# Two decays placed ahead of a weight rounding on ScalarE, and the second head sum of each pair placed behind the chunk's low products on TensorE

## Chip, cores, metric

One core of a Trainium2 chip runs the whole program. The metric is the device time of one execution in microseconds. TensorE (PE) does the matrix products, VectorE (DVE), ScalarE (ACT) and GpSimd (POOL) the rest, SyncE (SP) starts most transfers. Each engine takes its instructions strictly in the order in which the program gives them to it; between engines only semaphores order the work.

## What is computed

Two blocks, one after the other, on 1024 tokens of width 1024. The change touches only the first block, which has two layers:

```python
def hybrid_layer(x, ...):
    h = rms_norm(x, pre_gain) * (1.0 + scale) + shift
    proj = h @ w_in                     # 24 chunks of 128 columns, and a gate of rank 16
    (aq, ak, av, ag, rq, rk, rv, rg, gq, gk, gv, gg, ga) = jnp.split(proj, IN_SPLITS, axis=-1)
    a_out = sliding_window_attention(aq, ak, av, sinks) * jax.nn.silu(ag)
    r = retention(rq, rk, rv)
    r_out = rms_norm(r) * jax.nn.silu(rg)
    log_a = jax.nn.log_sigmoid(ga @ gla_gate_w + gla_gate_b) / 16
    g = gated_linear_attention(gq, gk, gv, log_a)
    g_out = rms_norm(g, gla_norm_gain) * jax.nn.silu(gg)
    y = jnp.concatenate([a_out, r_out, g_out], axis=-1) @ w_out
    return x + gate * rms_norm(y, post_gain)
```

The second block (attention over a window and a context, a gating unit, a Fourier mix and a wide feed-forward part) is not touched.

## The kernel before

**Units and chunks.** The first block runs as four units (`it` 0 to 3: two layers by two halves of 512 tokens). A unit goes through 32 weight chunks of 128 output columns: chunks 0 to 23 are the input projection, 24 to 31 the output projection. The products are made in a split float32 form: the raw chunk (`wraw`) is rounded on ScalarE to `whi` (`split_high`, line 620), GpSimd makes the rest `wlo` (`split_low`, line 523), and the PE makes three passes: `whi` with `h_hi` and with `h_lo` (`high_products`, line 1160, 16 matmuls of 512 columns), then `wlo` with `h_hi` (`low_products`, line 1168, 8 matmuls). "The third pass" of the change is `low_products`. `wraw`, `whi`, `wlo` and the result banks `lin0`, `lin1` have two places each, so a chunk's rounding waits until the PE has made the high products of the chunk two before (`hi_used`). Chunks 2 and 3, and 6 and 7, are made in pairs by `token_half` (line 1183): the first half in step 2, the second, with the release of both chunks, in step 3.

**The mixers.** Between the passes stand small steps of attention, retention and gated linear attention (GLA), placed by hand through a number `at`: position `2*s` stands ahead of chunk `s`, position `2*s+1` in its middle, between its high and its low products on the PE. On ScalarE the order of one step `s` is: `mixers(2s)`, `refill(s)` (the rounding of chunk `s+2`; at `s` = 3 of chunks 4 and 5, at `s` = 2 nothing), `mixers(2s+1)`, `evacuate(s)` (the result bank to SBUF, which frees it). Each engine has its own `mixers` function with the same numbers.

**Around the first part of the change (step 3 of a unit).** `log_decay` on ScalarE (position 4) and `log_sums` on VectorE (position 5) give `bsum`, the running sum of the gate's logarithms. GpSimd's `distance(0)` and `distance(1)` (position 6, line 538) write differences of it to `zed`. ScalarE's `decay(lv)` (lines 671 and 672) takes absolute value and exponential of `zed`; GpSimd's `keys(lv)` (line 549) and VectorE's `queries(lv)` (line 920) multiply with it, and the PE's `level(lv)` (line 1241) multiplies keys with queries. `level(0)` stands at position 8, between the modulation products of step 4 (`mod_products`, line 187) and the high products of chunk 4. Those wait also for ScalarE's evacuation of the bank of step 3 (line 768).

**Around the second part (steps 15, 16 and 19, 20).** The four 128-wide parts of the retention and GLA outputs are normalized over each head. `head_squares` makes squares. On the PE `head_sum(n)` (line 1335, one float32 matmul of 512 columns, recorded as two) sums them over a head into the single bank `bankM`. ScalarE's `head_root(n)` reads it with a logarithm (line 643); for odd `n` two exponentials follow (line 648), which need another activation table. VectorE's `head_scale` (line 967) multiplies, for both parts of a pair, at the odd position. `HEAD_SUM_AT = [30, 31, 38, 39]`: the first of a pair ahead of chunk 15 (19), the second in its middle. `head_sum(1)` may write `bankM` only when ScalarE has read the first sum (`head_log`). `mod_step` at the head of step 16 (20) writes `bankM` too, and waits for the logarithm of the second sum:

```python
if n in (0, 2):
    pe.wait_ge(*mod_out.after(it * mod_groups + HEAD_SUM_AT[n] // 8, 1))
else:
    pe.wait_ge(*head_log.after(it, n))
```

On VectorE `denominator` (line 992), which GpSimd's `normalized` (line 565) and then the PE's `turn_probs` in the middle of the next chunk (line 1364) wait for, stands behind the `head_scale` steps. ScalarE's `exponentials` (attention, position 30 and 38) stand ahead of `head_root`.

Of the kernel before, what the change touches and what calls it, by code (L numbers as in the profile page):

```python
# [38 lines left out]
LOGIT_AT, DIAG_AT = 4, 6  # L39
# [8 lines left out]
HEAD_SUM_AT = [30, 31, 38, 39]  # L48
# [317 lines left out]
def first_block(nc, t, a, sem):  # L366

    with ExitStack() as ctx:
# [99 lines left out]
        def group_of(it, s):  # L468

            return it * mod_groups + s // 4  # L470
# [140 lines left out]
        def _(act):  # L611
# [46 lines left out]
            def log_decay(it):  # L658

                l = it // NB  # L660
                act.wait_ge(*logit_done.after(it, 1))
                act.wait_ge(*h_ready.after(it, KB))
                link(nc.scalar.activation(zed[:, 0, :], four[0], ACT.Identity, bias=cols1[:, l, C_GB:C_GB + 1]))
                link(nc.scalar.activation(zed[:, 1, :], zed[:, 0, :], ACT.Abs))
                link(nc.scalar.activation(zed[:, 1, :], zed[:, 1, :], ACT.Exp, scale=-1.0))
                nc.scalar.activation(zed[:, 1, :], zed[:, 1, :], ACT.Ln, bias=1.0).then_inc(*sig_ready.one)
# [47 lines left out]
            def mixers(it, at):  # L714

                if at == LOGIT_AT - 1:
                    act.wait_ge(*ga_done.after(it, 1))
                    nc.scalar.activation(ga[:], bankE[0:2 * GATE_RANK, :], ACT.Copy).then_inc(*ga_ready.one)
                if at == LOGIT_AT:
                    log_decay(it)  # L720
                if at == DIAG_AT + 1:
                    decay(it, 0)
                    decay(it, 1)
                if at in LEVEL_AT:
                    lv = LEVEL_AT.index(at)
                    if lv + 2 <= LEVELS:
                        decay(it, lv + 2)
                    if lv == 2:
                        nc.scalar.activation(eb, bsum[:], ACT.Exp).then_inc(*eb_ready.one)
                        nc.scalar.activation(elast[:], bsum[:, P - 1::P], ACT.Exp).then_inc(*eb_ready.one)  # L730
                if at in FINAL_AT:
                    gla_final(it, FINAL_AT.index(at))
                if at == FINAL_AT[-1] + 2:
                    act.wait_ge(*g_evac.after(it, NT))
                    head_squares(it, 0)
                if at in RET_AT[1:]:
                    m = RET_AT.index(at) - 1
                    act.wait_ge(*r_out.after(it, m + 1))
                    nc.scalar.activation(rq[:, :, m * P:(m + 1) * P], bankE[:, 0:256].rearrange("p (c n) -> p c n", n=P),
                                         ACT.Copy).then_inc(*r_evac.one)  # L740
                if at == RET_AT[-1] + 2:
                    act.wait_ge(*r_evac.after(it, NT))
                    act.wait_ge(*kh_done.after(it, NT))
                    head_squares(it, 2)
                if at in SCORE_AT:
                    exponentials(it, SCORE_AT.index(at))
                if at in HEAD_SUM_AT:
                    head_root(it, HEAD_SUM_AT.index(at))
                if at == V_AT:
                    act.wait_ge(*v_turned.after(it, 1))  # L750
                    act.wait_ge(*carried.after(it, 1))
                    nc.scalar.activation(av[:, 1:, :].rearrange("p t n -> p (t n)"), bankE[:], ACT.Copy).then_inc(*v_ready.one)
                if at in TURN_AT:
                    transposed(it, TURN_AT.index(at))
# [52 lines left out]
            for it in range(UNITS):  # L807
# [19 lines left out]
                for k in range(KB):  # L827
                    s = OUT1 + k
# [321 lines left out]
        def _(pe):  # L1150
# [13 lines left out]
            def low_products(it, c):  # L1164

                pe.wait_ge(*w_split.after(it, c + 1))
                for k in range(KB):
                    last = nc.tensor.matmul(bank[c % 2], wlo[:, c % 2, k * P:(k + 1) * P], h_hi[:, k, :],  # L1168
                                            start=False, stop=(k == KB - 1))
                last.then_inc(*lin_done.one)  # L1170
# [157 lines left out]
            def head_sum(it, n):  # L1328

                pe.wait_ge(*head_sq_ready.after(it, n + 1))  # L1330
# [4 lines that stand above are left out]
                nc.tensor.matmul(bankM[:], ones64[:], head_sq[HEAD_ORDER[n]], start=True, stop=True).then_inc(*head_summed.one)  # L1335
# [56 lines left out]
            def mod_step(it, s):  # L1392

                g = group_of(it, s)
                if s % 4 < 2:
                    if s % 4 == 0 and g:
                        pe.wait_ge(*mod_out.after(g - 1, 1))
                        for n in (1, 3):
                            if s == HEAD_SUM_AT[n] // 2 + 1:
                                pe.wait_ge(*head_log.after(it, n + 1))  # L1400
                    for c in (2 * (s % 4), 2 * (s % 4) + 1):
                        pe.wait_ge(mod_in[c], 16 * (g + 1))
                        mod_products(nc, bankM, c * P, cact, mod_ring, c).then_inc(*mod_summed.one)
                elif s in FOLD_AT:
                    pe.wait_ge(*mod_row_ready.after(g, 1))
                    fold_products(nc, bankM[:, 0:4 * VEC * MOD_GROUP], t["fold"][:], mod_row[:]).then_inc(*mod_turned.one)

            def mixers(it, at):

                if at == 2:  # L1410
                    gate_rank(it)
                if at == LOGIT_AT:
                    pe.wait_ge(*ga_ready.after(it, 1))
                    nc.tensor.matmul(four[0], t["gate_w"][:, it // NB, :], ga[:], start=True, stop=True).then_inc(*logit_done.one)
                if at == DIAG_AT:
                    diagonal(it)
                if at in LEVEL_AT:
                    level(it, LEVEL_AT.index(at))
                if at in FINAL_AT:
                    gla_final(it, FINAL_AT.index(at))  # L1420
                if at in RET_AT:
                    retention(it, RET_AT.index(at))
                if at in HEAD_SUM_AT:
                    head_sum(it, HEAD_SUM_AT.index(at))
                if at == V_AT:
                    turn_values(it)
                if at in SCORE_AT:
                    score(it, SCORE_AT.index(at))
                if at in TURN_AT:
                    turn_probs(it, TURN_AT.index(at))  # L1430
                if at in VALUE_AT:
                    values(it, VALUE_AT.index(at))

            x_summed(0)
            for it in range(UNITS):
                for s in range(OUT1):
                    mod_step(it, s)
                    mixers(it, 2 * s)
                    if s in (GV, RV):
                        token_half(it, s, 0)  # L1440
                    elif s in (GV + 1, RV + 1):
                        token_half(it, s - 1, 1)
                    else:
                        high_products(it, s, when=(lambda k: h_ready.after(it, k + 1)) if s == 0 else None)
                        if it and s == 0:
                            y_summed(it - 1)
                        mixers(it, 2 * s + 1)
                        low_products(it, s)
                mod_step(it, OUT1)
                mixers(it, 2 * OUT1)  # L1450
                for c in range(2):
                    pe.wait_ge(*lin_free.after(it, OUT1 + c + 1))
                    pe.wait_ge(*w_split.after(it, OUT1 + c + 1))
                    out_products(it, c, MIX_ORDER[:4])
                mod_step(it, OUT1 + 1)
                for c in range(2):
                    out_products(it, c, MIX_ORDER[4:])
                for k in range(2, KB):
                    mod_step(it, OUT1 + k)
                    if k == 5:  # L1460
                        x_summed(it + 1)
                    if k < KB - 1:
                        high_products(it, OUT1 + k)
                        low_products(it, OUT1 + k)
                    else:
                        last_products(it, OUT1 + k)
# [1730 lines left out]
```

## Time and profile before

| | before |
|---|---|
| median of 3 runs | 4014.93 us |
| lowest and highest | 4013.55, 4018.3 us |
| the profiled execution, whole time | 4015.34 us |
| its span, first to last instruction | 4013.6 us |
| PE busy | 93% of the span |
| mean granted clock of the PE | 0.97 |
| first block, four units | about 76 to 1243 us of the span |

All times below are microseconds from the start of the span. An engine's idle time stands in a row in brackets, with the engine and line that ended it. PEclk is the PE's granted clock: 1.00 is 2.4 GHz, and where it falls it falls to 1.2 GHz for a stretch.

### The profile page before, as it was taken

To read this page: it belongs to the slowest core of one execution; us is meant where nothing else is said; L and a number is where in the kernel's file an instruction comes from. 1 tells how busy PE (TensorE), PEld (TensorE's weight loads), DVE (VectorE), ACT (ScalarE), POOL (GpSimd) and SP (SyncE) were. 2 spreads that over 40 slices of the span, in tenths; PEclk is the share of its full clock that TensorE was granted. 3 is DMA by queue.
4 is the path that set the end of the run, shared out by engine and by line. 5 is a ranking of instruction groups with operands and counts; after the bars stand their busy time and mean duration, and the time that the engine had idled before them with its cause. 6 is when DMAs were issued, how large, how long until landed. Compare 5 with 4: busy or idle time off the path is not lost.

```text
span 4013.6 us, 61376 instructions
## 1 busy us (share of the span) xinstructions
PE 3716.5 (93%) x22388; PEld 2993.7 (75%) x22388; DVE 2118.4 (53%) x3355; ACT 1726.9 (43%) x2899; POOL 1779.6 (44%) x1288
## 2 busy tenths in 40 slices
PE   4999999999998899888999999999899899999997
PEld 3767767767766677657888898887777778887886
DVE  5546546546546567667324655236667574235234
ACT  2355355355355544555223454235444553233223
POOL 1543544434443522325455885454322355455444
PEclk7999999999999899998999999999999999999999
DMA  6333433433333321212232453322221223232323
GB/s 252 122 124 125 138 118 126 146 111 134 127 122 109 103 82 48 64 53 87 91 98 92 145 173 110 94 94 79 85 84 53 63 79 94 89 96 96 94 92 103
DMA packets 127222, 421.32 MB, mean 105 GB/s; under 512 B 17281, under 2 KB 19105, under 8 KB 126369
## 3 DMA queue, kind: packets, MB, share of 16 engines
q1 hardware_dynamic: 121488, 410.09, 31.1%
q10 hardware_dynamic: 5520, 8.34, 0.6%
q8 instruction: 140, 2.29, 0.2%
q14 instruction: 74, 0.60, 0.0%
HBM read 397.40 MB, written 6.29 MB: 101 GB/s over the span
## 4 chain that ended last, share of the span: by engine, by line
PE 54%; DVE 7%; ACT 3%; issue 2%; POOL 0%; DMA 0%; SPq 0%; ACTq 0%; DVEq 0%; POOLq 0%
PE lin L2672 30%; PE lin L2681 15%; PE bankO L2797 2%; PE lin L2930 2%; PE bankT L2739 2%; DVE x L2317 1%; DVE tmp L2283 1%; DVE y L2316 1%; PE scores L2772 1%; DVE h_lo L2306 1%; DVE staged L2295 1%; PE lin L2814 1%; ACT whi L1902 0%; PE lin L2702 0%; PE scores L2773 0%
## 5 line engine op out<-in xcount | busy, mean ns | idle before, releaser
L1883 POOL TENSOR_TENSOR wlo<-late_raw,whi 128x512 fp32r<-128x512 f32 x456 | 641.2, 1429 | 764.4 <-PE lin L2681 497.6
L1883 POOL TENSOR_TENSOR wlo<-wraw,whi 128x512 fp32r<-128x512 f32 x452 | 635.9, 1431 | 716.8 <-PE lin L2681 497.5
L2672 PE MATMUL lin<-h_hi,whi 128*128 128x512 f32 (+1 forms) x1896 | 715.2, 384 | 47.4 <-ACT f L2196 12.4
L2672 PE MATMUL lin<-h_lo,whi 128*128 128x512 f32 (+1 forms) x1896 | 701.1, 377 | 0.0
L523 POOL TENSOR_TENSOR wlo<-wraw,whi 128x512 fp32r<-128x512 f32 x260 | 359.5, 1404 | 464.6 <-PE lin L1168 290.2
L2672 PE MATMUL lin<-a_hi,whi 128*128 128x512 f32 (+1 forms) x1280 | 471.9, 376 | 12.0 <-ACT tmp L2205 7.8
L2672 PE MATMUL lin<-a_lo,whi 128*128 128x512 f32 (+1 forms) x1280 | 468.7, 374 | 0.0
L2672 PEld LDWEIGHTS lin<-h_hi,whi 128*128 128x128 f32 x1896 | 368.2, 194 | 133.5 <-issue 24.9
L1902 ACT ACTIVATE whi<-late_raw 128x1024 fp32r<-128x1024 f32 x228 | 239.2, 1057 | 517.2 <-PE lin L2672 414.9
L1902 ACT ACTIVATE whi<-wraw 128x1024 fp32r<-128x1024 f32 x226 | 237.3, 1057 | 497.0 <-PE lin L2672 413.3
L2681 PE MATMUL lin<-h_hi,wlo 128*128 128x512 f32 (+1 forms) x1896 | 439.8, 375 | 1.2 <-POOL wlo L1883 0.8
L2672 PEld LDWEIGHTS lin<-h_lo,whi 128*128 128x128 f32 x1896 | 368.7, 194 | 61.1 <-issue 1.2
L2681 PEld LDWEIGHTS lin<-h_hi,wlo 128*128 128x128 f32 x1896 | 334.0, 190 | 66.6 <-issue 6.2
L2550 DVE TENSOR_TENSOR tmp<-tmp 128x512 f32<-128x512 f32 (+1 forms) x160 | 185.3, 1158 | 335.3 <-ACT tmp L2205 330.2
L1160 PE MATMUL lin<-h_hi,whi 128*128 128x512 f32 x800 | 334.9, 419 | 10.5 <-DVE h_lo L869 10.5
L1160 PE MATMUL lin<-h_lo,whi 128*128 128x512 f32 x800 | 323.4, 404 | 0.0
L2681 PE MATMUL lin<-a_hi,wlo 128*128 128x512 f32 (+1 forms) x1280 | 296.9, 376 | 2.1 <-POOL wlo L1883 2.1
L2672 PEld LDWEIGHTS lin<-a_hi,whi 128*128 128x128 f32 x1280 | 241.9, 189 | 67.2 <-ACT tmp L2205 15.7
L2672 PEld LDWEIGHTS lin<-a_lo,whi 128*128 128x128 f32 x1280 | 242.0, 189 | 46.2 <-issue 0.2
L620 ACT ACTIVATE whi<-wraw 128x1024 fp32r<-128x1024 f32 x130 | 136.7, 1057 | 302.6 <-PE lin L1160 206.6
L2576 DVE TENSOR_TENSOR y<-lin,y 128x512 f32 (+1 forms) x96 | 66.4, 692 | 378.4 <-PE lin L2681 378.2
L2681 PEld LDWEIGHTS lin<-a_hi,wlo 128*128 128x128 f32 x1280 | 226.7, 190 | 51.3 <-POOL wlo L1883 3.4
(381 smaller groups left out, 6435.4 us busy)
## 6 DMA issues: line engine op xcount, KB each, us to landing
wraw<-in_w SPq DMA_DIRECT2D x332, 512.0 KB, 3.5
late_raw<-in_w SPq DMA_DIRECT2D x212, 512.0 KB, 3.5
mod_ring<-in_w_ada SPq DMA_DIRECT2D x96, 512.0 KB, 4.6
mod_ring<-in_w_mod SPq DMA_DIRECT2D x32, 512.0 KB, 4.6
tmp<-tmp SPq DMA_DIRECT2D x224, 64.0 KB, 2.0
first_ring<-in_w_mod SPq DMA_DIRECT2D x16, 512.0 KB, 16.6
wraw<-in_dft_tokens SPq DMA_DIRECT2D x16, 512.0 KB, 3.5
late_raw<-in_dft_tokens SPq DMA_DIRECT2D x16, 512.0 KB, 3.5
```

The source lines that it names most:

```text
L523: last = nc.gpsimd.tensor_tensor(wlo[:, s, half], wraw[:, s, half], whi[:, s, half].bitcast(F32), ALU.subtract)
L620: nc.scalar.activation(whi[:, s, :], wraw[:, s, :], ACT.Copy).then_inc(*w_hi.one)
L1160: last = nc.tensor.matmul(bank[c % 2], whi[:, c % 2, k * P:(k + 1) * P], h[:, k, :], start=(k == 0 and h is h_hi), stop=False)
L1883: last = nc.gpsimd.tensor_tensor(wlo[:, s, half], raw_chunk[r][:, half], whi[:, s, half].bitcast(F32), ALU.subtract)
L1902: nc.scalar.activation(whi[:, s, 0:D], raw_chunk[r], ACT.Copy).then_inc(*w_hi.one)
L2550: nc.vector.tensor_tensor(tmp[:, 2 + s, 0:w], tmp[:, 4 + s, 0:w], tmp[:, 4 + s, 0:w], ALU.mult).then_inc(*a_sq.one)
L2576: nc.vector.tensor_tensor(part, bank[s][:, 0:p.w], part, ALU.add).then_inc(*lin_free.one)
L2672: last = nc.tensor.matmul(bank[s][:, 0:p.w], whi[:, s, k * P:(k + 1) * P], h[:, k, 0:p.w], start=(k == 0 and h is parts[0]), stop=False)
L2681: last = nc.tensor.matmul(bank[s][:, 0:p.w], wlo[:, s, k * P:(k + 1) * P], parts[0][:, k, 0:p.w], start=False, stop=(k == KB - 1))
L2739: last = nc.tensor.transpose(out, probs[i % 2][:, kv, k * P:(k + 1) * P], ident[:])
L2797: last = nc.tensor.matmul(bankO[half, g * P:(g + 1) * P], v, probsT[:, kv, at:at + P], start=(k == 0), stop=(k == n - 1))
L2930: return nc.tensor.matmul(bank[c][:, 0:2 * P].rearrange("p (t n) -> p t n", t=2), x_part[:, k, cols], w[:, 0:2, k * P:(k + 1) * P], start= ...
```

## The change

Three lines of order are changed, nothing of what is computed. On ScalarE `decay(it, 0)` and `decay(it, 1)` move from position 7 to position 6 of a unit, that is from behind the rounding of chunks 4 and 5 to ahead of it. On the PE the second `head_sum` of each pair moves from the middle of chunk 15 (19) to behind that chunk's low products. At position 39 `turn_probs` and `values` of attention stand in the middle of the chunk as before.

```diff
@@ ScalarE, mixers
-                if at == DIAG_AT + 1:
+                if at == DIAG_AT:
                     decay(it, 0)
                     decay(it, 1)
@@ TensorE, mixers
-                if at in HEAD_SUM_AT:
+                if at in HEAD_SUM_AT[::2]:
                     head_sum(it, HEAD_SUM_AT.index(at))
@@ TensorE, the loop over the chunks
                         mixers(it, 2 * s + 1)
                         low_products(it, s)
+                        if 2 * s + 1 in HEAD_SUM_AT:
+                            head_sum(it, HEAD_SUM_AT.index(2 * s + 1))
```

## Rows read from the trace of the kernel before

**Rows 1.** The page's first part: busy time, share, instructions of each engine.

```profile
PE 3716.5 (93%) x22388; PEld 2993.7 (75%) x22388; DVE 2118.4 (53%) x3355; ACT 1726.9 (43%) x2899; POOL 1779.6 (44%) x1288
```

**Rows 2.** Waits of the PE in 80 to 1240: total us, times, longest.

```profile
PE bankM L1335 <- ACT tmp L643: 19.7, 8, 2.5
PE bankM L195 <- DVE mod_row L1050: 14.9, 8, 2.9
PE quad L1241 <- POOL big L549: 11.1, 4, 2.8
```

**Rows 3.** Timeline of ScalarE, unit 1, step 3: start us, us, line, operation.

```profile
395.94 2.00 ACT L620 ACTIVATE whi<-wraw 128x1024 fp32r<-128x1024 f32 x2 [7.27 <-PE lin L1183]
397.86 0.62 ACT L671 ACTIVATE big<-big 128x512 f32<-128x512 f32 x1
398.49 1.28 ACT L672 ACT_TABLE_LOAD   x1
...
400.96 0.63 ACT L672 ACTIVATE big<-big 128x512 f32<-128x512 f32 x1
401.50 1.07 ACT L768 ACTIVATE gv<-lin 128x512 f32<-128x512 f32 x2
```

**Rows 4.** Timeline of GpSimd and VectorE in the same stretch.

```profile
392.32 2.07 POOL L538 TENSOR_TENSOR big<-bsum 128x512 f32<-128x512 f32 x2 [5.21 <-DVE bsum L900]
...
400.49 0.73 POOL L549 TENSOR_TENSOR big<-gk,big 128x256 f32<-128x256 f32 x1 [6.09 <-ACT big L672]
400.52 2.39 DVE L920 TENSOR_TENSOR tmp<-gq,big 128x256 f32<-128x256 f32 x2 [4.74 <-ACT big L672]
```

**Rows 5.** Timeline of the PE: unit 1's modulation products, unit 0's first product of chunk 4.

```profile
397.75 1.08 PE L187 MATMUL bankM<-mod_ring,cact 128*32 128x128 f32 x32
...
113.03 0.50 PE L1160 MATMUL lin<-h_hi,whi 128*128 128x512 f32 x1
```

**Rows 6.** Busy times by stretch (stretch, length, engines, PEclk, DMA share, GB/s), level(0) to level(1); last row level(2) to level(3).

```profile
111.98:118.50 6.52, 6.52 (x49) 5.06 (x49) 3.59 (x3) 2.23 (x4) 6.52 (x6) 0.74 0.24 83
401.60:409.28 7.68, 7.68 (x48) 6.10 (x49) 4.02 (x3) 2.23 (x4) 7.68 (x8) 0.61 0.22 73
...
983.19:989.66 6.47, 6.47 (x48) 5.04 (x48) 3.54 (x3) 2.23 (x4) 6.47 (x6) 0.74 0.22 81
122.61:127.52 4.91, 4.91 (x52) 3.90 (x48) 2.77 (x2) 1.88 (x4) 4.91 (x6) 1.00 0.45 114
```

**Rows 7.** Timeline of all engines around unit 0's first pair of head sums.

```profile
220.94 0.60 ACT L643 ACTIVATE tmp<-bankM 128x512 f32<-128x512 f32 x1
221.44 1.05 ACT L620 ACTIVATE whi<-wraw 128x1024 fp32r<-128x1024 f32 x1
...
221.68 1.10 PE L1335 MATMUL bankM<-tmp,ones 128*128 128x512 f32 x2 [2.47 <-ACT tmp L643]
...
222.22 2.42 PE L1168 MATMUL lin<-h_hi,wlo 128*128 128x512 f32 x8
...
222.82 0.60 ACT L643 ACTIVATE tmp<-bankM 128x512 f32<-128x512 f32 x1 [0.33 <-PE bankM L1335]
...
224.57 1.08 PE L187 MATMUL bankM<-mod_ring,cact 128*32 128x128 f32 x32
...
227.37 1.89 POOL L565 TENSOR_TENSOR big<-big,rden 128x1024 f32<-128x1024 f32 x1 [11.27 <-DVE rden L995]
...
230.43 1.04 PE L1364 MATMUL quad<-ident,big 128*128 128x128 f32 x8
```

**Rows 8.** Busy by stretch: second pairs, the same without head sum, unit 0's first pair.

```profile
258.66:267.60 8.94, 6.48 (x27) 4.07 (x27) 1.73 (x5) 6.74 (x11) 0.00 (x0) 0.81 0.24 99
...
1131.43:1140.48 9.05, 6.59 (x28) 4.14 (x27) 2.31 (x5) 6.75 (x11) 0.75 (x1) 0.81 0.00 0
273.44:277.46 4.02, 4.02 (x25) 2.70 (x24) 1.62 (x4) 2.34 (x7) 1.89 (x1) 1.00 0.93 368
219.21:224.57 5.36, 2.89 (x12) 1.81 (x11) 0.88 (x2) 4.98 (x8) 0.00 (x0) 1.00 0.10 38
```

## The prediction

> **What bounds the kernel now.** I read four views, in this order. The page's busy times: the PE is busy for 93% of the span, no other engine for more than 53% [rows 1]. So time is won only where the PE stands still or runs slow, and only if nothing else is late right behind. Second, the list of the PE's waits inside the first block's units. Two of its lines belong to the change: the second head sum waits for ScalarE's logarithm of the first (line 643), 8 times, 19.7 us together; and level(0) waits for GpSimd's keys (line 549), 4 times, 11.1 us [rows 2]. A third line (14.9 us, the fold for VectorE's transposed row) is not touched, but shows that other stalls stay. Third, the timelines around both stalls, to see what the late engine did before. Fourth, the busy times by stretch, for the granted clock: it is 0.74, 0.61 and 0.74 in the stretches that begin with the stalled level(0), and 1.00 in the stretch two levels on [rows 6]. The PE falls to 1.2 GHz during or just behind such a stall, and the reader is to see that a stall costs more than its own length.
>
> **Part 1, the decays.** ScalarE stood idle for 7.27 us before it rounded chunks 4 and 5, released by the PE's pair of chunks 2 and 3 at 395.94 [rows 3]. The input of decay(0) was there long before: GpSimd made both distances from 392.32 in 2.07 us, so the first was ready at about 393.4 and the second at 394.4 [rows 4]. That is 2.6 us before the roundings could begin. The decays take from 397.86 to 400.96 + 0.63 = 401.59, so 3.73 us with one table load of 1.28 [rows 3]. Moved ahead they run from 393.4 to 397.1. They issue no transfer and are moved past the roundings alone.
>
> *What the PE gains.* The exponential of decay(0) ends at 393.4 + 0.62 + 1.28 + 0.63 = 395.9. GpSimd has been idle since 394.4 (6.09 us before 400.49) and makes the keys in 0.73; VectorE has been idle since 395.8 (4.74 us before 400.52) and makes its queries in about 1.2 [rows 4]. Both are there by 397.2. The PE ends its modulation products at 397.75 + 1.08 = 398.8 [rows 5] and finds no wait. The stall of 2.76 to 2.77 goes in each unit: **11.1 us**.
>
> *What is queued behind.* The roundings now wait for the decays: 397.1 instead of 395.94, 1.2 us late, and end at 399.1; the first bank of step 3 is evacuated 0.6 us later, at 399.7. Level(0) takes 113.03 - 111.98 = 1.05 us of the PE [rows 5, 6], so chunk 4 can begin at 398.8 + 1.05 = 399.9 at the earliest: 0.2 us of slack, less the 0.1 that a semaphore needs. I cost this at nothing; without that cover it costs what the decays are late, at most 1.2 us in a unit. GpSimd's low part of chunk 4 follows the rounding, from 398.2 to 400.9, and is wanted by the third pass some 4.7 us behind the start of chunk 4. GpSimd's later distances and keys move up with it by about 3 us, while the PE moves up by more, so their distance shrinks by a microsecond; no level has waited for them behind level(0), and I see none that would.
>
> *The clock.* Level(0) to level(1) took 6.52, 7.68 and 6.47 us in units 0, 1 and 3 (unit 2 is as unit 0), at a clock of 0.74 or 0.61. The same work, one small product set and 16 matmuls and what is between, took 4.91 at full clock [rows 6]. If the fall goes with the stall, 1.61 + 2.77 + 1.61 + 1.56 = **7.5 us** come back. Bounds: nothing, if the PE falls anyway, and 7.5. I take 7.5, because the nearest like stretch (modulation products, then a level, without a wait) holds 1.00 (the last row of [rows 6]).
>
> *A rule of the notes.* In the trace the exponential starts as soon as the load of 1.28 us ends, and the load directly behind the absolute value [rows 3]. The Trainium skill ("ScalarE: Activation LUTs", What ACT_TABLE_LOAD costs) gives 1283 ns for the load and about 1380 ns more for a drain at each switch. By that rule the roundings would be 1.4 us later still, chunk 4 would wait about 1.3 us in three units, and the change would bring 4 us less. No such drain is to be seen here.
>
> **Part 2, first pair (steps 15, 16).** The PE was done with the high products at 221.68 - 2.47 = 219.2. The third pass, moved ahead, is 2.42 us as recorded at most (about 2.0 from start to start) and hides all but a few tenths of the wait, which still ends at 221.54 with the first logarithm (220.94 + 0.60) [rows 7]. The head sum therefore stands where it stood, at about 221.7, and so do ScalarE's second logarithm (222.82 to 223.42), its exponentials, VectorE's scalings and GpSimd's normalization. But now step 16's modulation products are right behind the head sum, and they wait for that second logarithm, which the third pass hid before. They start 0.1 behind it, at 223.5, where they had started at 224.57. The gain is 1.04 and not 2.47; four times: **4.2 us**. The wait of 0.7 us that is left is the one that takes the place of the old.
>
> **Part 2, second pair (steps 19, 20).** Here attention's turn_probs and values stand in the middle of the chunk too, and now run ahead of the wait. From the last high product to the modulation products the PE took 8.94 us in unit 0 and 9.05 in unit 3 (9.04 and 9.05 between), at a clock of 0.81. The same without a head sum took 4.02 at full clock, from 273.44 [rows 8]. To this come the head sum, 1.10, 0.04 to the logarithm, its 0.60, and 0.1 for the semaphore [rows 7]: 4.02 + 1.85 = 5.87. The first logarithm is over by then (it released the old wait 2.46 us behind the high products, the new place is 4.0 behind them), so nothing else is waited for. Gain 36.08 - 4 x 5.87 = **12.6 us**, of which 6.3 is the clock (8.94 - 2.46 - 4.02 - 0.95 = 1.5, and 1.6 three times, 0.95 being what a head sum holds the PE at full clock). Bounds of that clock part: nothing and 6.3; I take 6.3 since 1.7 us less stand idle in one piece.
>
> *What is late next.* The PE's turn_probs in the middle of chunk 16 (20) waits for GpSimd's normalization. In the first pair that ended at 227.37 + 1.89 = 229.26, 5.84 behind the second logarithm. The PE reaches it 230.43 - 224.57 = 5.86 behind its modulation products [rows 7], in the second pair 273.44 - 267.60 = 5.84 [rows 8]; and these now start 0.1 behind the logarithm. So both arrive together within 0.1 us. Before, the PE came about 1.1 us after the normalization. I cost this at nothing, with up to 1 us at each of 8 places as its bound; it caps any further gain. ScalarE's second logarithm is 0.6 us later in the second pair, and the bank that it evacuates behind it is wanted only a chunk later.
>
> **Sum.** 11.1 + 7.5 + 4.2 + 12.6 = 35.4 us of the profiled execution: 4015.34 - 35.4 = 3979.9. The median of the runs stands 0.4 lower: 3979.5. I forecast **3980**.
>
> **Rivals.**
> 1. *The clock falls as often as before*, or falls in the new places: behind the change a pair has a head sum, 0.7 us idle, modulation products of 32 columns and scores of half the rows in a row. For it: the PE gets no dense work for about 4 us there. Against it: the old wait of 2.47 us in the first pair, with the same small work around, kept 1.00 in unit 0 (the last row of [rows 8]). Without any clock gain the time is 4014.9 - (35.4 - 7.5 - 6.3) = 3993; with falls only at the eight pairs (6.3 lost and four new ones of 1.6) 3992.
> 2. *The race at turn_probs is lost* by some tenths up to a microsecond, from VectorE or GpSimd, whose shared work stretches their instructions: 8 x 0.5 = 4 up to 8 us, and perhaps 1 us in each unit where chunk 4 waits for the late rounding: 3984 to 3992.
> 3. *More falls vanish or appear elsewhere*: the fold's stall of 2.9 us stays, and everything behind the first unit starts at other moments. A fall more or less is 1.6 us; I allow three either way: 3975 to 3985.
> 4. *The first part does nothing*, because the distance isn't ready before the roundings. Then ScalarE waits for GpSimd and rounds late. The row says 2.6 us early. If it came at the moment of the old roundings, level(0) would find its keys 2 us earlier than before but chunk 4 would wait for the roundings: part 1 about zero, 3998.
> 5. *Slower than before*: the roundings of chunks 4 and 5, and the head sums behind the low products, hold up more than they free. One mechanism decides: ScalarE takes work in order, so each microsecond that the distances are late holds both roundings, and chunk 4 with them. From a distance later than about 393.6 the PE begins to pay; for the whole gain of a unit (4.6 us, and part 2's 4.2 with it) it would have to be ready about 9 us later, at 402, which nothing in the trace comes near. With it the time would be 4016 to 4025.
>
> **Chances.** The sum as worked out, with the shifts of rival 3: 0.62. Rival 1: 0.13. Rival 2: 0.16. Rival 4: 0.03. More than 40 us of gain: 0.02. Rival 5 and everything of no effect or worse: 0.04. The range that should hold 8 in 10 goes from 3974 (three falls fewer) to 3994 (no clock gain). A measurement of this kernel can tell about 0.2%, 8 us, from no change: faster 0.95, within it 0.03, slower 0.02.
>
> **What would show it.** Right: in the list of the PE's waits level(0) behind GpSimd's keys is gone; the head sum's wait falls from 2.5 to about 0.4 in the first pairs and vanishes in the second, and a new wait of about 0.7 us, 8 times, stands before the modulation products behind line 643; level(0) to level(1) is 4.9 us at 1.00; last high product to modulation products is 4.3 us in the first pairs and 5.9 in the second. Wrong: a wait before chunk 4's first product behind ScalarE's line 768 or 620, a wait of turn_probs behind GpSimd's line 565, or a clock below 1.00 in those stretches. The second block should take the same time.

## The result

| | before | after |
|---|---|---|
| median of the runs shown with the result | 4014.3 us (4 runs) | 3983.69 us (4 runs) |
| lowest and highest | 4013.55, 4018.3 | 3981.6, 3987.18 |
| profiled execution, span | 4013.6 us | 3985.4 us |
| first block, first product to the second block's first | 1166.35 us | 1136.66 us |
| second block | 2770.8 us | 2772.1 us |

The changed kernel is faster by 30.6 us; the ratio is 0.9926, with a 95% interval of 0.9914 to 0.9938. On another chip, over 5 runs, it took 3984.73 against 4015.67, the same ratio. Single executions of one kernel lie up to 14 us apart (the kernel before: 4005.61 to 4019.89 over 20 runs there), so a few microseconds between two medians say little, and the readings below rest on rows.

The list of the PE's waits in the units of the first block, kernel after (total us, times, longest; it answers to [rows 2]):

```profile
PE bankM L195 <- DVE mod_row L1050: 15.0, 8, 2.9
...
PE bankM L187 <- issue: 5.9, 8, 0.7
PE lin L1160 <- DVE h_lo L869: 3.7, 6, 0.7
PE bankE L1380 <- ACT av L752: 2.9, 4, 0.7
PE bankM L1335 <- ACT tmp L643: 2.6, 4, 0.7
PE lin L1183 <- POOL wlo L523: 1.2, 4, 0.3
```

The wait of level(0) is gone. The head sum waits 0.7 us instead of 2.5, and only in the first pairs. Two waits are new: the one in front of the modulation products (line 187, 0.7 us, 8 times, that for the second logarithm) was forecast, the one in front of attention's values (line 1380, for ScalarE's copy of V) was not. Two small ones grew: chunk 0's products wait for VectorE's low part of the input (line 869) for 3.7 us instead of 1.5, and chunk 7 for its low weights (line 523) for 1.2 instead of 0.3.

The step of the decays in unit 1, kernel after: timelines of ScalarE and GpSimd (they answer to [rows 3, 4]).

```profile
387.40 0.63 ACT L671 ACTIVATE big<-big 128x512 f32<-128x512 f32 x1 [4.79 <-POOL big L538]
...
390.53 0.63 ACT L672 ACTIVATE big<-big 128x512 f32<-128x512 f32 x1
391.07 1.99 ACT L620 ACTIVATE whi<-wraw 128x1024 fp32r<-128x1024 f32 x2
392.96 1.06 ACT L768 ACTIVATE gv<-lin 128x512 f32<-128x512 f32 x2
...
390.06 0.74 POOL L549 TENSOR_TENSOR big<-gk,big 128x256 f32<-128x256 f32 x1 [1.66 <-ACT big L672]
```

The decays start as soon as the first distance is there and end at 391.16; the keys are ready at 390.8. The PE, for which the same stretch looks like this, asks for them only at 392.70 and goes on into chunk 4 at once:

```profile
391.69 1.08 PE L187 MATMUL bankM<-mod_ring,cact 128*32 128x128 f32 x32
392.70 1.12 PE L1241 MATMUL quad<-tmp,big 32*128 32x64 f32 x32
393.75 0.50 PE L1160 MATMUL lin<-h_hi,whi 128*128 128x512 f32 x1
```

The busy times by stretch, kernel after: level(0) to level(1) in units 1 and 3, and from chunk 19's turn_probs to the modulation products of step 20 in unit 0 (they answer to [rows 6, 8]). The last number but two is PEclk.

```profile
392.72:397.61 4.89, 4.89 (x54) 3.90 (x51) 1.33 (x1) 2.41 (x5) 4.89 (x5) 1.00 0.34 108
959.16:964.06 4.90, 4.90 (x54) 3.91 (x50) 1.33 (x1) 2.41 (x5) 4.90 (x5) 1.00 0.32 107
255.90:261.58 5.68, 4.95 (x27) 3.11 (x26) 0.00 (x0) 4.02 (x8) 0.00 (x0) 1.00 0.40 168
```

All of it runs at 2.4 GHz. The first pair of unit 0, kernel after, timeline (it answers to [rows 7]):

```profile
218.68 0.60 ACT L643 ACTIVATE tmp<-bankM 128x512 f32<-128x512 f32 x1
...
219.42 1.10 PE L1335 MATMUL bankM<-tmp,ones 128*128 128x512 f32 x2 [0.66 <-ACT tmp L643]
220.55 0.60 ACT L643 ACTIVATE tmp<-bankM 128x512 f32<-128x512 f32 x1 [0.33 <-PE bankM L1335]
...
221.25 1.08 PE L187 MATMUL bankM<-mod_ring,cact 128*32 128x128 f32 x32 [0.73 <-issue]
...
225.10 1.89 POOL L565 TENSOR_TENSOR big<-big,rden 128x1024 f32<-128x1024 f32 x1 [11.27 <-DVE rden L995]
...
227.08 1.06 PE L1364 MATMUL quad<-ident,big 128*128 128x128 f32 x8
```

From the head sum to the modulation products it is 221.25 - 219.42 = 1.83 us, where it was 2.89. GpSimd's normalization ends at 226.99 and turn_probs starts at 227.08: the two arrive together.

The new wait for V's copy, one chunk on in unit 0: timelines of the kernel before, then of the kernel after.

```profile
234.93 2.51 POOL L523 TENSOR_TENSOR wlo<-wraw,whi 128x512 fp32r<-128x512 f32 x2
237.68 0.16 DVE L986 SCALAR_TENSOR_TENSOR nmax<-mx,cols 128x4 f32<-128x4 f32 x1
239.98 0.61 ACT L752 ACTIVATE av<-bankE 128x512 f32<-128x512 f32 x1
240.73 1.08 PE L1380 MATMUL bankE<-big,av 128*64 128x256 f32 x8
```

```profile
233.90 1.29 POOL L523 TENSOR_TENSOR wlo<-wraw,whi 128x512 fp32r<-128x512 f32 x1
234.35 0.86 DVE L986 SCALAR_TENSOR_TENSOR nmax<-mx,cols 128x4 f32<-128x4 f32 x1
237.35 0.61 ACT L752 ACTIVATE av<-bankE 128x512 f32<-128x512 f32 x1
238.10 1.08 PE L1380 MATMUL bankE<-big,av 128*64 128x256 f32 x8 [0.73 <-ACT av L752]
```

The copy stands behind exponentials, these need VectorE's line 986, and that needs scores which the PE made. So this chain moves up with the PE: line 986 starts 3.33 us sooner (237.68 to 234.35). But GpSimd's low part (line 523) moves up by 2.3 us only and ends at 235.19; the small VectorE instruction now starts inside it and ends at 235.21, after 0.86 us instead of 0.16. The 0.70 us are what values then waits. The copy had been done 0.1 us before turn_probs ended (240.59 and 240.69), so there was no slack to take them up.

**Where the 29.7 us of the first block come from.** The stalls of level(0), 11.1. The clock in level(0) to level(1), 27.2 us over the four units before (unit 2 is as unit 0) and 19.6 after, 7.6. The first pairs, 4.2. The second pairs, 14.0. That is 36.9. Given back: 2.7 net for V's copy; about 0.6 for the low part of chunk 7; 1.5 for a fall of the clock behind the fold's stall in unit 0, where there was none; and 2.4 for falls at the start of units 2 and 3, which came at worse moments. 36.9 - 7.2 = 29.7. The second block took 1.3 us more in this execution.

The start of unit 3, from its first modulation products to the next ones, before and after:

```profile
944.08:954.84 10.76, 10.57 (x59) 7.23 (x59) 8.25 (x11) 3.79 (x6) 2.67 (x2) 0.71 0.39 146
921.71:933.68 11.97, 10.65 (x58) 7.42 (x58) 8.27 (x11) 3.78 (x6) 2.69 (x2) 0.71 0.38 131
```

The granted clock is 0.71 in both. Before, the first modulation products ran at 0.50 and took 1.93 us. After, they ran at 1.00 and took 1.08; the PE then stood 1.3 us idle instead of 0.2, waiting for VectorE's low part of the input, and the fall met the products of chunk 0 behind that wait.

### The profile page after: what moved, and what is told of

The parts are those of the page before. It is cut to its first block, busy times and chain, and to the rows that moved or that the text cites. A ratio compares the mean times of both kernels' runs of the same rounds, so it can differ in the third digit from the quotient of the medians.

```text
span 3985.4 us, 61376 instructions
## 1 busy us (share of the span) xinstructions
PE 3701.6 (93%) x22388; PEld 2990.2 (75%) x22388; DVE 2124.2 (53%) x3355; ACT 1725.2 (43%) x2899; POOL 1777.2 (45%) x1288
## 4 chain that ended last, share of the span: by engine, by line
PE 54%; DVE 7%; ACT 3%; issue 2%; POOL 0%; DMA 0%; SPq 0%; ACTq 0%; DVEq 0%; POOLq 0%
PE lin L2674 30%; PE lin L2683 15%; PE bankO L2799 2%; PE lin L2932 2%; PE bankT L2741 2%; DVE x L2319 1%; DVE tmp L2285 1%; DVE y L2318 1%; PE scores L2774 1%; DVE h_lo L2308 1%; DVE staged L2297 1%; ACT whi L1904 1%; PE lin L2816 1%; PE lin L2704 0%; PE scores L2775 0%
## 5 line engine op out<-in xcount | busy, mean ns | idle before, releaser
L2674 PE MATMUL lin<-h_hi,whi 128*128 128x512 f32 (+1 forms) x1896 | 714.9, 384 | 48.9 <-ACT f L2198 12.6
```

The lines of the kernel that those rows point to most:

```text
L2674: last = nc.tensor.matmul(bank[s][:, 0:p.w], whi[:, s, k * P:(k + 1) * P], h[:, k, 0:p.w], start=(k == 0 and h is parts[0]), stop=False)
```

## The experiments

All were timed against the kernel before in five rounds, each group of kernels on one chip; medians stand beside the kernel before's on the same chip (4016.1, 4015.67 and 4015.56 us in the three groups, on three chips).

**Each part alone.** The decays alone:

```diff
-                if at == DIAG_AT + 1:
+                if at == DIAG_AT:
                     decay(it, 0)
                     decay(it, 1)
```

> The kernel before with the first part of the change alone: the two decays ahead of the roundings. Theory: the wait of level(0) for the keys goes (11.1 us) and the clock's fall behind it goes with it, so level(0) to level(1) is 4.9 us at a granted clock of 1.00 in all units: 18.6 to 19 us less in the first block, less 0.6 for a short wait of chunk 7 for its low part that the changed kernel shows (0.3 a unit, half of it paid); no wait at the values step of chunk 17, because the PE reaches it no sooner after the second logarithm than before. About 3996, give or take 3 for falls of the clock elsewhere. Rival (the falls of the clock are not tied to the stall): 11 us less, 4003, and a clock below 1.00 in those stretches.

Measured: 4002.78 against 4016.1, ratio 0.9965 (0.9952 to 0.9979), 13.3 us less. The stall of level(0) is gone and level(0) to level(1) is 4.9 us at 1.00 in all four units:

```profile
109.54:114.44 4.90, 4.90 (x60) 3.94 (x52) 1.33 (x1) 1.65 (x4) 4.90 (x5) 1.00 0.31 104
396.98:401.87 4.89, 4.89 (x60) 3.96 (x52) 1.32 (x1) 2.41 (x5) 4.89 (x5) 1.00 0.30 101
```

So both terms of part 1 are there. But 5 us of the 18.7 don't arrive. The time is not the expected 3996 but the rival's 4003; the rows above refute the rival all the same, since the clock in these stretches is 1.00. The rows of the first pairs, whose stalls of 2.5 us this kernel still has, show where some go: behind the head sum, where the kernel before held 1.00, the clock falls in units 0 and 3:

```profile
219.30:223.40 4.10, 3.74 (x10) 2.51 (x10) 0.00 (x0) 3.74 (x6) 0.00 (x0) 0.71 0.01 4
1079.43:1083.49 4.06, 3.71 (x10) 2.51 (x10) 0.00 (x0) 3.70 (x6) 0.00 (x0) 0.72 0.00 0
```

These two cost 1.2 us each. From the fold of step 14 to the next head sum unit 0 has a new fall too (7.4 us for 5.8), unit 1 a longer one (8.7 for 7.4), unit 2 none (5.8 for 7.4), and the start of unit 3 takes 1.2 us more.

The second part alone, both head sums moved and the decays as before:

> The kernel before with the second part alone: the second head sum of both pairs behind the third pass. Theory: 4.2 us from the first pairs and 13.9 from the second, as between the two traces, less 2.7 for the wait of the values step of chunk 17 for ScalarE's copy of V, which appears when the PE comes 1.06 us sooner while ScalarE doesn't: 15.4 less, about 3999. Rival (the wait for V's copy comes from the first part of the change, which moves the PE ahead of ScalarE as a whole): no such wait here, 18 less, 3996.

Measured: 3997.12, ratio 0.9956 (0.9943 to 0.9970), 19 us less by the medians and 17 by the means. Its list of waits has the wait for V's copy:

```profile
PE quad L1241 <- POOL big L549: 11.0, 4, 2.8
...
PE bankE L1380 <- ACT av L752: 2.9, 4, 0.7
```

so that wait belongs to the second part, and the rival that put it down to the first falls. The two parts together give 13 + 19 = 32 us, the change 31: they add up, as far as medians that stray by some microseconds can say.

**The two pairs apart.** The head sum moved in the first pair alone:

```diff
-                if at in HEAD_SUM_AT:
+                if at in HEAD_SUM_AT and at != HEAD_SUM_AT[1]:
                     head_sum(it, HEAD_SUM_AT.index(at))
...
                         low_products(it, s)
+                        if 2 * s + 1 == HEAD_SUM_AT[1]:
+                            head_sum(it, HEAD_SUM_AT.index(2 * s + 1))
```

> The kernel before with the head sum moved in the first pair alone (chunk 15). Theory of the prediction: 1.04 us less to the modulation products of step 16 in each unit (4.2), all of it traded for an idle wait of 0.7 us that is left there; and 2.7 of the 4.2 are given back at the values step of chunk 17, which waits for ScalarE's copy of V: 1.5 less, about 4014. Rival (the clock, which holds 1.00 in the first pair, falls less often once the stall is shorter): 4 to 8 us less, 4008 to 4012.

Measured: 4015.11 against 4015.67, ratio 1.0005 (0.9996 to 1.0014): nothing. The PE is ahead by 1.06 us at step 16, and waits for V's copy one chunk later (2.8 us in all). The second pair alone (the same edit with `HEAD_SUM_AT[3]`):

> The kernel before with the head sum moved in the second pair alone (chunk 19). Theory: 3.4 to 3.5 us a unit, of which 1.5 is the clock that no longer falls behind the stall; 13.9 us less, about 4002, no wait for V's copy. Rival (the gain of the second pair needs the first pair's move): under 10 us less.

Measured: 4002.61, ratio 0.9971 (0.9962 to 0.9981), 13.1 us less, without a wait for V's copy. So the second part's gain is all from the second pair, where attention's steps fill the wait.

**The clock, with the stall left in place.** Here 11 products whose result is thrown away fill the PE's stall in the kernel before:

```diff
+                if at == LEVEL_AT[0]:
+                    for k in range(11):
+                        nc.tensor.matmul(bankE[0:2 * GATE_RANK, :], t["ga_both"][:, KB * (it // NB) + k % KB, :], h_hi[:, k % KB, :],
+                                         start=True, stop=True)
                 if at in LEVEL_AT:
                     level(it, LEVEL_AT.index(at))
```

> The kernel before, with 11 idle products of 32 by 512 columns put into the PE's stall ahead of level(0) (their result is thrown away; nothing else is changed, the decays stand where they stood). They fill about 2.6 us of the 2.8 that the PE stands still, so the wait is not shortened, only filled. Theory that the fall of the clock comes from the idle PE: level(0) starts when it started, within 0.2 us, and level(0) to level(1) falls from 6.5 or 7.7 to 4.9 us in all units: 7.5 us less, about 4007. Rival (the fall comes from something else there, such as the many small products ahead of and behind the stall): same clock of 0.74, time as before, 4014 to 4015.

The rows agree with the theory in all four units (two shown; timeline of the PE, then busy times by stretch):

```profile
108.92 1.08 PE L187 MATMUL bankM<-mod_ring,cact 128*32 128x128 f32 x32
109.93 2.74 PE L1419 MATMUL bankE<-h_hi,ga_both 128*32 128x512 f32 x11
112.78 0.96 PE L1241 MATMUL quad<-tmp,big 32*128 32x64 f32 x25
```

```profile
112.70:117.60 4.90, 4.82 (x48) 3.94 (x48) 2.62 (x2) 1.61 (x4) 4.90 (x5) 1.00 0.24 74
401.73:406.62 4.89, 4.82 (x48) 3.94 (x48) 2.62 (x2) 1.60 (x4) 4.89 (x5) 1.00 0.22 69
```

Level(0) starts where it started, 3.86 us behind the modulation products, and the stretch behind it takes 4.9 us instead of 6.5 and 7.7. So the fall of the clock comes from the idle PE, and 7.5 us of this term are a matter of the clock alone. One row elsewhere shows that a stall brings the fall almost always and not always: in unit 0 of the kernel with the second part alone level(0) waits 2.8 us and the stretch behind it still takes 4.9 us at 1.00.

The expected time did not come: 4021.29 us, ratio 1.0015 (1.0006 to 1.0024). The first block is only 4.1 us shorter in its profile. The 7.5 are there, but a fall behind unit 0's fold costs 1.6, the starts of units 2 and 3 cost 1.1 to 1.2 more each, and chunk 7 waits longer for its low weights (1.7 us in all instead of 0.3), while unit 1 has one fall fewer at the fold and the pairs. The untouched second block took 2779.8 us against 2770.8. There it is not the clock, whose mean is 0.98 in both, and not the work (PE busy for 2608.5 us and 2608.9): the PE stood idle for 9 us more, in waits for VectorE and ScalarE. Why those came later was not found; it stays open.

**V's copy.** In the changed kernel ScalarE copies V behind the exponentials of position 34, of which values needs nothing. The copy is put ahead of them:

```diff
+                if at == V_AT:
+                    act.wait_ge(*v_turned.after(it, 1))
+                    act.wait_ge(*carried.after(it, 1))
+                    nc.scalar.activation(av[:, 1:, :].rearrange("p t n -> p (t n)"), bankE[:], ACT.Copy).then_inc(*v_ready.one)
                 if at in SCORE_AT:
                     exponentials(it, SCORE_AT.index(at))
                 if at in HEAD_SUM_AT:
                     head_root(it, HEAD_SUM_AT.index(at))
-                if at == V_AT:
...
```

> The changed kernel with ScalarE's copy of V ahead of the exponentials of position 34 and not behind them. Theory: the copy is then done about 2 us sooner, the wait of 0.7 us at the values step of chunk 17 goes in all four units, 2.9 us less than the changed kernel: about 3981. Rival (the PE then meets another wait right behind, such as the probabilities of the next step, which now come 0.6 us later): no gain against the changed kernel, 3984.

Measured: 3986.67 against 4016.1, ratio 0.9928, no better than the changed kernel. The wait is gone all the same; values follows turn_probs directly (timeline of the PE):

```profile
236.28 1.04 PE L1364 MATMUL quad<-ident,big 128*128 128x128 f32 x8
237.25 1.08 PE L1380 MATMUL bankE<-big,av 128*64 128x256 f32 x8
```

What took the 3 us is seen from the fold of step 14 to the head sum of step 15 in unit 1, by stretch, first the changed kernel, then this one:

```profile
486.77:494.18 7.41, 7.41 (x27) 6.05 (x28) 2.65 (x7) 1.63 (x3) 0.31 (x1) 0.77 0.67 231
```

```profile
485.22:493.83 8.61, 8.61 (x26) 6.93 (x27) 2.65 (x7) 1.64 (x3) 0.31 (x1) 0.65 0.54 199
```

The same work takes 5.8 us where the clock holds 1.00 (207.47 to 213.28 before). Here the fall behind the fold's stall lasted longer, at a granted clock of 0.65 against 0.77. Units 2 and 3 show the same (8.7 and 8.8 us for 7.4), so the three cost 3.9 us. Why the falls were longer was not found. That is the rival's result by another way than the rival's: no new wait, a longer fall.

**The stall that was left.** The fold of step 14 waits 2.9 us for VectorE's transposed row, which stood behind retention and rope steps. VectorE was idle ahead of them:

```diff
+                    if s == 13:
+                        mod_rows(it, s)
                     mixers(it, 2 * s + 1)
-                    if s % 4 == 1:
+                    if s % 4 == 1 and s != 13:
                         mod_rows(it, s)
```

> The changed kernel with one further edit: VectorE's transposed row of step 13 stands ahead of the retention and rope steps of position 27 and not behind them. VectorE was idle for 4.7 us there. Theory that stalls of the PE and the falls of its clock behind them are what is left: the wait of 2.9 us at the fold of step 14 goes in all four units (11.7 us) and the fall behind it, 1.6 us or more each (6.6): 3966 to 3969. Rival (the steps behind, head sum and scores, wait for VectorE instead, whose rope steps stay where they are): the gain is under 6 us, 3978 or more.

Measured: 3962.38 against the changed kernel's 3984.73 in the same group, ratio to before 0.9876 (0.9860 to 0.9891): 22 us for one moved instruction per unit, and more than the 16 to 19 expected. In the profiled executions the first block is 19.8 us shorter than the changed kernel's (1116.9 us for 1136.7); another 7 us of that profile lie in the second block, where nothing was edited. The waits of 2.9 us are gone and no fall follows there, in any of the four units. Timeline of VectorE and, from the busy times by stretch, fold to head sum in unit 0:

```profile
194.51 0.61 DVE L958 SCALAR_TENSOR_TENSOR rstate<-rstate,ret_cdecay,rnew 128x128 f32<-128x128 f32 x2
195.16 0.72 DVE L1050 STREAM_TRANSPOSE mod_row<-bankM 128x512 f32<-128x512 f32 x1
199.74 0.42 DVE L955 TENSOR_TENSOR rnew<-quad,ones 128x256 f32<-128x256 f32 x1 [3.87 <-PE bankE L1326]
```

```profile
201.60:207.32 5.72, 5.72 (x28) 4.73 (x27) 3.86 (x8) 2.22 (x4) 3.09 (x2) 1.00 0.38 85
```

Once more, and beside it the kernel with both further edits:

> The kernel with the transposed row first once more, as the partner of the next one on the same chip. Both theories: 3960 to 3966.

> The changed kernel with both further edits: the copy of V ahead of the exponentials, and the transposed row of step 13 first. Theory (the copy's 3.1 us are real, and were hidden in the run with that edit alone by longer falls of the clock behind the fold's stall, which is gone here): no wait for V's copy, 3 us less than its partner without that edit, 3958 to 3961. Rival (the wait moves to another place): no difference from the partner.

Measured: 3966.3 and 3958.65 against 4015.56; ratios 0.9875 (0.9859 to 0.9890) and 0.9851 (0.9836 to 0.9866). The rows show what V's copy is worth with the fold's stall gone: values comes 0.7 to 0.8 us sooner in each unit than in the first run of the partner, 3.1 us in all, and no fall behind the fold takes it back. The medians lie 7.7 us apart, but with four runs each their intervals touch, so no more than the 3 us is shown. The kernel with both edits is the fastest, 57 us below the kernel before and some 26 below the changed one, which ran on another chip.

**How much slack the late rounding has.** The changed kernel with 1.3 us of needless work between the decays and the roundings:

```diff
                     decay(it, 0)
                     decay(it, 1)
+                    for _ in range(2):
+                        link(nc.scalar.activation(eb, bsum[:], ACT.Exp))
```

> The changed kernel with 1.3 us of needless work on ScalarE (two exponentials whose result is written again later by the kernel itself) between the decays and the roundings of chunks 4 and 5. Theory of the prediction, that chunk 4 has 0.2 us of slack in units 1 to 3 and about 1.1 in unit 0: chunk 4's first product waits for ScalarE's evacuation (line 768) by about 1.1 us in three units and 0.2 in the first, 3.5 us more than the changed kernel, 3988, and the clock doesn't fall. Rival (the slack is larger than worked out, because the PE has other work to hide it): no wait and no difference, 3985.

Measured: 3990.57, ratio 0.9932 (0.9919 to 0.9946). The list of waits has the new line, and the PE's timeline shows it in unit 1:

```profile
PE lin L1162 <- ACT gv L770: 3.1, 3, 1.0
```

```profile
393.26 1.12 PE L1243 MATMUL quad<-tmp,big 32*128 32x64 f32 x32
395.40 0.50 PE L1162 MATMUL lin<-h_hi,whi 128*128 128x512 f32 x1 [1.03 <-ACT gv L770]
```

Of 1.28 us of delay 1.03 arrive at the PE in units 1 to 3 and nothing that is listed in unit 0. The slack is 0.25 us, as worked out. The time is 2.6 us above the expected 3988, on a chip where the changed kernel did not run.

The changed kernel once more, beside the kernels of the second group:

> The changed kernel once more, on the same chip as the three that follow, since single executions of one kernel lie up to 14 us apart with the clock's falls. Both theories: 3984 to 3987, and the waits as in the first trace of the changed kernel.

Measured: 3984.73 us, 3981.41 to 3990.95, with the same waits.

## Why the prediction was right, point by point

*What bounds.* Right: the PE's stalls and the falls of its clock behind them carried the whole gain, and the next stall of the same list, once removed, gave some 20 us more.

*Part 1, the stall.* Right to the tenth: the decays start with the distance and end 3.76 us later, the keys are ready 1.9 us before the PE asks for them, level(0) starts at once. 11.1 us, and the rows of the decays alone show the same.

*Part 1, what is queued behind.* Right: no wait of chunk 4, with 0.25 us of slack measured against 0.2 worked out.

*Part 1, the clock.* Right in its place: 7.6 us against 7.5, and the filler shows the idle PE as the cause. Incomplete as a sum. I took falls as fixed to their stalls and let them vanish one by one. The kernel with the decays alone has falls in first pairs that the kernel before did not have, behind the same stall of 2.5 us; the changed kernel has one more behind the fold in unit 0 and later ones at the starts of units 2 and 3. A stall of 2.5 to 2.9 us makes a fall likely; whether it comes and how long it lasts differs between executions with the same stall, and no run shows what decides it. Rival 3 had this, with 5 us either way; it cost 3.9.

*The drain after a table load.* The trace after decides against it again: behind the absolute value at 387.40 the exponentials and their load end at 391.16, 3.76 us for all, as in [rows 3]. With 1.4 us more in each unit chunk 4 would have waited, as it did when ScalarE was given 1.3 us more.

*Part 2, first pair.* The mechanism and the size at its place are right: 1.06 us against 1.04, and the old wait traded for two of 0.7. (The first of them was forecast at 0.4; the moment of the head sum hangs on the logarithm, so this costs nothing.) The step that failed is "What is late next". It looked at turn_probs in chunk 16, where both sides arrive together as forecast (0.09 us apart), and stopped there. One chunk on, attention's values wait for ScalarE's copy of V. The copy's chain moved up with the PE. GpSimd did not gain the 1.06 us, since its work hangs, through VectorE's denominators, on the second logarithm; so VectorE's line 986 now falls into its line 523 and lasts 0.7 us longer. In the nine profiled executions with the first pair moved it takes 0.80 to 0.86 us in all four units and ends 0.02 us behind line 523; in the four others it takes 0.16 to 0.17. No run moves GpSimd's work alone, so the coincidence is shown and its reason is not. That gave back 2.7 of the 4.2 us, and with the first pair alone nothing at all can be measured.

*Part 2, second pair.* Right, and undersized: 3.4 to 3.5 us a unit, 14.0 in all, against 12.6. The term was mis-sized at both ends: the high products' end was read from the recorded end of the last one, which lies 0.16 us behind the moment at which the next could start, and the head sum with the wait behind it is 5.68 - 4.02 = 1.66 us and not 1.85.

*The sum.* 35.4 forecast; 36.9 where I looked, 7.2 given back where I didn't, 29.7 in the first block, 30.6 by the medians. The range held because it took in lost tenths at eight places and falls elsewhere; what came was one lost wait at a place that none of the rivals named, and falls that one of them did. Rival 2 did not come true at turn_probs; what it named as the cause, shared work of VectorE and GpSimd that stretches an instruction, is what the rows show one chunk on. Rivals 1, 4 and 5 did not come true. That the time came within 4 us of the forecast is in part luck: the second pairs' 1.4 us too little and the terms that were missing stand against each other, and each part alone missed its own expectation, one by 7 us and one by 2.

## What to carry to other kernels

When a stall goes, follow the engine that is now early through every wait of the next chunks until one has more slack than was won: a wait that was met by a tenth is not in the list of waits. Look as well at what did not move up: an engine that stays behind is then busy at other moments of the chain, as GpSimd was here. Moving work into a wait pays in full only where other work is already there to follow it, as in the second pair; where the next step hangs on the same result, as in the first, little is left. And read the stall and the clock behind it as one price: here a stall of 2.8 us at level(0) cost 4.4 to 5.5 us and the fold's of 2.9 us between 2.9, where no fall came, and 5.9, so the largest left in the list of waits is as a rule worth more than its length.

## What the runs showed of the hardware

A fall of the PE's clock to 1.2 GHz came behind stalls of 2.5 to 2.9 us, but not each time: behind the first head sum never in the kernel before and twice in the kernel with the decays alone, at the same length of stall. Counted over all profiled executions here, four units each, the clock fell behind level(0)'s stall of 2.8 us in 15 of 16 stretches, behind the fold's of 2.9 us in 31 of 40, behind that of 2.5 us in the second pairs in 15 of 16, and behind that of 2.5 us in the first pairs in 5 of 16. Where the stall was gone, filled or cut to 0.7 us it was 1.00 in each of these stretches: 36 at level(0), 12 at the fold, 36 and 36 at the pairs. Filling the stall with products of 32 columns was enough to keep 2.4 GHz. The three lengths of the stretch from the fold to the next head sum (16 high and 8 low products and what is around them), 5.8, 7.4 and 8.6 us, show no fall, a fall, and a longer one.

A VectorE instruction of 128x4 elements (line 986) took 0.16 to 0.17 us in 16 cases where GpSimd's subtraction of line 523 had ended before it, and 0.80 to 0.86 us, to 0.02 us behind the end of that subtraction, in 36 cases where it started inside it.

The second block, untouched, took between 2764.8 and 2779.8 us in the profiled executions of the kernels here. The longest is that of the kernel with the filler, with 9 us more of idle PE at the same clock, and the reason was not found.
